# Gate and value of the state output from high and low parts, made by VectorE as the state output leaves its banks

## The reference, cut to what matters

```
y = jax.nn.gelu(s5_ssm(u, ...))              # (1, 1024, 256), "the state output"
ya, yb = jnp.split(y @ w_glu[l], 2, axis=-1) # w_glu: (256, 512)
o_ssm = ya * jax.nn.sigmoid(yb) * jax.nn.silu(z_ssm)
```

## Time and profile before

| | |
|---|---|
| median of 3 runs | 935.52 us (935.25 to 935.66) |
| profiled execution | 934.83 us, of which span 932.9 us |
| TensorE busy | 893.1 us, 96% |
| VectorE busy | 525.2 us, 56% |
| ScalarE busy | 416.9 us, 45% |
| GpSimd busy | 210.5 us, 23% |

### The profile page before, as it was taken

How to read it: one execution, slowest core, us unless ns; L and a number is a source line. 1 busy time by engine, 2 the same in 40 slices (tenths; PEclk the granted TensorE clock), 3 DMA queues, 4 the chain that set the end, 5 groups by cost and what they waited for, 6 DMA issues and landing times. The chain is left out here.

```text
span 932.9 us, 14437 instructions
## 1 busy us (share of the span) xinstructions
PE 893.1 (96%) x5577; PEld 735.0 (79%) x5577; DVE 525.2 (56%) x1098; ACT 416.9 (45%) x828; POOL 210.5 (23%) x203
## 2 busy tenths in 40 slices
PE   2799999999999999999999999999999999999997
PEld 2478999789999777777777776888888888887885
DVE  3652374359665697797798796732223122237454
ACT  6732232522345478778778768621111111133221
POOL 3359812111000103212212212255652000000000
PEclk9999999999999999999999999999999999999998
DMA  9956052041010000000000001333232121133222
GB/s 300 332 154 97 5 117 69 1 95 46 1 47 1 1 1 1 2 1 1 1 1 1 2 1 35 86 96 96 63 107 69 38 55 36 59 123 136 90 91 91
DMA packets 61092, 59.46 MB, mean 64 GB/s; under 512 B 10240, under 2 KB 53824, under 8 KB 61008
## 3 DMA queue, kind: packets, MB, share of 16 engines
q1 hardware_dynamic: 58768, 53.90, 20.1%
q0 software_dynamic: 2000, 4.54, 1.8%
q10 hardware_dynamic: 256, 0.09, 0.0%
HBM read 52.69 MB, written 5.24 MB: 62 GB/s over the span
## 5 line engine op out<-in xcount | busy, mean ns | idle before, releaser
L1240 DVE TENSOR_TENSOR plo<-pt,phi 128x512 fp32r<-128x512 f32 x192 | 106.2, 567 | 37.0 <-ACT phi L849 36.6
L849 ACT ACTIVATE pt<-bank 128x512 f32<-128x512 f32 (+1 forms) x208 | 99.6, 479 | 51.4 <-PE bank L1769 50.8
L1769 PE MATMUL bank<-q,k 128*128 128x512 f32 (+3 forms) x384 | 102.4, 348 | 0.4 <-ACT phi L849 0.4
L849 ACT ACTIVATE phi<-bank 128x512 fp32r<-128x512 f32 (+1 forms) x208 | 99.6, 479 | 0.0
L1769 PEld LDWEIGHTS bank<-q,k 128*128 128x128 f32 x384 | 63.0, 189 | 13.4 <-ACT phi L849 4.1
L648 POOL TENSOR_TENSOR qa<-qa,otmp 128x256 f32<-128x256 f32 x32 | 27.2, 851 | 198.4 <-DVE otmp L1240 198.4
L1562 DVE TENSOR_REDUCE mx<-slc_max 128x1 f32<-128x128 f32 (+3 forms) x64 | 48.2, 753 | 11.1 <-PE slc_max L1769 9.3
L1769 PE MATMUL bank<-ht_hi,dhi 128*128 128x512 f32 x128 | 49.8, 389 | 0.0
L1769 PE MATMUL bank<-ht_lo,dhi 128*128 128x512 f32 x128 | 49.8, 389 | 0.0
L1769 PE MATMUL bank<-ht_hi,dlo 128*128 128x512 f32 x128 | 49.8, 389 | 0.0
L1240 DVE TENSOR_TENSOR dtm<-bank,dsig 128x512 f32<-128x512 f32 x16 | 11.1, 691 | 64.4 <-ACT dsig L849 64.4
(11 more groups left out here) (445 smaller groups left out, 2600.6 us busy)
## 6 DMA issues: line engine op xcount, KB each, us to landing
ada<-in_w_ada SPq DMA_DIRECT2D x16, 512.0 KB, 10.1
draw<-in_w_in SPq DMA_DIRECT2D x16, 512.0 KB, 4.0
wraw<-in_w_in SPq DMA_DIRECT2D x7, 1024.0 KB, 5.7
xs<-in_x SPq DMA_DIRECT2D x8, 512.0 KB, 8.5
gstage<-in_w_ada POOLq DMA_DIRECT2D x16, 256.0 KB, 3.0
oraw<-in_w_out SPq DMA_DIRECT2D x8, 512.0 KB, 6.6
xr<-in_x SPq DMA_DIRECT2D x8, 512.0 KB, 4.2
out<-yr SPq DMA_DIRECT2D x7, 512.0 KB, 2.9
```

Of the source, the lines that this page charges most:

```text
L849: return nc.scalar.activation(o, i, fn, **kw)
L1240: return V.tensor_tensor(o, a, b, op)
L1769: return T.matmul(o, l, r, start=start, stop=stop, **kw)
```

## The change

TensorE's `glu` now makes each product from three pairs of fp32r matmuls (high weights x high output, low weights x high output, high weights x low output), twelve for a product where there were four in float32. VectorE makes the parts. In the step `("yt", 0)` it first makes those of the weights (`glu_weight_parts`: three copies, three subtractions), then in each step `("yt", q)` it waits for ScalarE's GELU of this quarter, copies it to `yt_hi` and writes `yt - yt_hi` to `yt_lo`, which lies in the place of `yt` itself (`state_rows_parts`). A new semaphore `early_lo`, which takes the place of `wlo0`, counts the first weights' low half, the weights' parts and the eight output parts, 10 in all. `glu(0)` waits for count 9 (the fourth high part) before its first matmul and for count 10 before its first matmul with a low output part. The wait of `glu(0)` for the weights' DMA moves to VectorE.

```diff
+    yt_hi = at("yt_hi", [P, 2, SEQ], R, R_K + 17408)
+    yt_lo = at("yt_lo", [P, 2, SEQ], R, R_Z)
+    wglu_hi = [[at("wglu_hi0", [P, 512], R, r_used - 2048)],
+               [at("wglu_hi1a", [P, 256], R, R_K + 16384), at("wglu_hi1b", [P, 256], R, R_K + 31744)]]
+    wglu_lo = at("wglu_lo", [P, 2, 512], R, R_K + 25600)
...
-                    .then_inc(once("wlo0") if half == 0 else s_wlo, 1)
+                    .then_inc(once("early_lo") if half == 0 else s_wlo, 1)
...
+            def glu_weight_parts():
+
+                dve.wait_ge(once("wglu"), 16)
+                pieces = ((0, 0, 0, 512), (1, 0, 0, 256), (1, 1, 256, 512))
+                for k, p_, c0, c1 in pieces:
+                    ch.mark(V.tensor_copy(wglu_hi[k][p_][:, :], wglu[:, k, c0:c1]))
+                ch.wait()
+                for k, p_, c0, c1 in pieces:
+                    ins = tt(wglu_lo[:, k, c0:c1], wglu[:, k, c0:c1], f(wglu_hi[k][p_][:, :]), ALU.subtract)
+                ins.then_inc(once("early_lo"), 1)
+
+            def state_rows_parts(q):
+
+                if q == 0:
+                    glu_weight_parts()
+                ctile, jh = divmod(q, 2)
+                part = lambda t: t[:, ctile, :].rearrange("p (n j) -> p j n", j=CH)[:, 4 * jh:4 * jh + 4, :]
+                dve.wait_ge(s_trf, first["yt"] + q + 1)
+                V.tensor_copy(part(yt_hi), part(yt)).then_inc(once("early_lo"), 1)
+                dve.wait_ge(once("early_lo"), 3 + 2 * q)
+                tt(part(yt_lo), part(yt), f(part(yt_hi)), ALU.subtract).then_inc(once("early_lo"), 1)
...
+                elif step[0] == "yt":
+                    state_rows_parts(step[1])
...
-                if n == 0:
-                    pe.wait_ge(once("wglu"), 16)
-                    pe.wait_ge(s_trf, first["yt"] + 4)
...
-                    for k in range(2):
-                        ins = mm(bank[2 + part], wglu[:, k, col:col + P], yt[:, k, cc * HALF:(cc + 1) * HALF],
-                                 k == 0, k == 1)
+                    w_high = (wglu_hi[0][0][:, col:col + P], wglu_hi[1][col // 256][:, col % 256:col % 256 + P])
+                    w_low = [wglu_lo[:, k, col:col + P] for k in range(2)]
+                    for m, (l, r) in enumerate(((w_high, yt_hi), (w_low, yt_hi), (w_high, yt_lo))):
+                        if n == 0 and part == 0 and m != 1:
+                            pe.wait_ge(once("early_lo"), 9 if m == 0 else 10)
+                        for k in range(2):
+                            ins = mm(bank[2 + part], l[k], r[:, k, cc * HALF:(cc + 1) * HALF],
+                                     m == 0 and k == 0, m == 2 and k == 1)
```

More of the change, by code:

```diff
@@ L1849, in _ @@
             pe.wait_ge(s_whi, 1)
-            pe.wait_ge(once("wlo0"), 1)
+            pe.wait_ge(once("early_lo"), 1)
             def state_input(k, cc):
```

## The result

The changed kernel takes 936.96 us (median of 19 runs, 935.96 to 937.97) beside 935.31 for the kernel before (19 runs, 934.89 to 936.45). The ratio is 1.0016 (95% interval 1.001 to 1.0023): 1.65 us slower, a change that can be told from none but lies within 0.2%. The spread of the changed kernel, 2.0 us, is wider. Its profiled execution took 935.99 us (span 934.2), near the lower end of its runs.

What follows compares the result with a forecast made beforehand. TensorE, busy 893.1 of 932.9 us, was taken to bound the kernel. A 4.5 us late start, less 2.84 gained, plus 1.7 for the clock made +3.4: 938.9 us, own range 937.5 to 940, wide range 933.3 to 940.6.

Steps and rivals of the forecast that it cites:

- the late start: TensorE's first product, waiting for VectorE's fourth high part, starts at 176.1 instead of 171.59: 4.5 us late.
- What is removed: On TensorE, twelve fp32r matmuls replace four float32 ones: 2.72 instead of 3.43 us a product, 2.84 for four.
- The weights' parts: VectorE's three copies and three subtractions for the weights end at about 168.1 in its hole and cost nothing.
- The subtraction: VectorE's subtraction for an output quarter, 512 elements at a step of 8 elements: 1.08 us.
- The copy: VectorE's copy of an output quarter, 512 elements at a step of 8 elements: 1.08 us.
- rival B: VectorE copies two elements at a time despite the step, 0.62 us: 935.5, or 937.2 with clock fall; chance 0.24.
- The clock: TensorE's pause of 4.3 us before the first product lets its clock fall to 1.2 GHz: 1.7 us lost.
- The sum: Over the whole kernel, 4.5 - 2.84 + 1.7 = +3.4 us, giving 938.9.
- The low part: TensorE's first product waits 0.2 us for the fourth low output part at full pace, not at the lower clock.
- C: The step costs VectorE nothing, copy 0.41 and subtraction 0.69 us: -2.2 us, 933.3; chance 0.18.
- C's dividing line: The change gains if VectorE's copy and subtraction for one output quarter take below some 1.9 us.
- Nothing downstream absorbs: No later TensorE wait in the stretch absorbs a shift; the hidden layer starts at 224.6, before 221.18.

Runs made afterwards that it cites:

- e3_warm: Changed kernel plus nine extra fp32r matmuls on TensorE ahead of the first product's wait, results overwritten: 935.32 us beside 935.06 for the kernel before.
- e5_gain: Kernel before with twelve fp32r matmuls a product; ScalarE writes the fp32r output itself, low output part left out: 932.26 us beside 934.88.
- e2_again: The changed kernel run once more, nothing altered: 937.08 us beside 935.06 for the kernel before.
- e6_wait: Changed kernel's VectorE instructions and first-product wait, but with the float32 products of the kernel before: 939.41 us beside 934.88 for the kernel before.
- e10_warm4: Changed kernel plus four extra fp32r matmuls on TensorE ahead of the first product's wait: 935.23 us beside 935.02 for the kernel before.
- e1_steps: Kernel before plus 13 VectorE copies and subtractions of 512 elements with various steps; only durations count: copy 0.42 in a row, subtraction 0.69.
- e4_rows: Changed kernel, VectorE splitting the output in contiguous halves, first product waiting for the third copy instead of the fourth: 932.51 us beside 935.06.
- e7_fill: Changed kernel with the projection of key tile 5 moved ahead of the first product on TensorE: 932.48 us beside 934.88 for the kernel before.
- e8_steps: Kernel before plus nine VectorE copies and subtractions of 512 elements with other steps; only durations count: all six subtractions 1.09 to 1.12 us.
- e9_both: Changed kernel with contiguous halves on VectorE and the projection of key tile 5 ahead of the first product: 932.18 us beside 935.02.

## Why the prediction was right in direction and off in size

Forecast were 938.9 us and +3.4; measured are 936.96 and +1.65. The direction holds, and so do the two mechanisms, a late copy and a fall of the clock; the size is twice too large. That the direction came out hangs on the clock. In the prediction the late start alone (4.5 us) outweighed the gain (2.84); measured, it doesn't (2.47), and with the clock kept up e3_warm is level with the kernel before. By the steps of the prediction:

- **What is removed.** A product in 2.72 us where it took 3.43: the second one measures 2.72, and e5_gain 2.62 us for the four with 2.84 forecast.
- **The weights' parts** end at 167.96 with 168.1 forecast and cost nothing.
- **The subtraction** at 1.08 us: 1.07 to 1.13.
- **The copy** at 1.08 us: here the prediction failed. It measures 0.62 to 0.67. I had both bounds and the right value, 0.62, under rival B, and took the rate of the subtraction because the nearest row with a step was a two-source instruction. The casts of the earlier trace rows had shown that a one-source instruction is not bound to that rate; the chance of 0.24 for B was too low. Four times 0.43 us too much, and 0.3 us of small sums, put the start of the first product at 176.1 instead of 174.06.
- **The clock.** Forecast was a fall in a pause of 4.3 us at 1.7 us; it fell in or behind one of 2.2 already and cost 1.5 and 1.7 us in two profiles, 1.8 between e2_again and e3_warm. That the price of 1.7 came out is in part luck: it was read from the pace of transposes in a stretch in which the granted clock on record stays 1.00. And the delay of 2.0 us from the earlier trace rows, by which a pause of 4.3 us was judged long, is 2.0 to 5.1 us in ten profiles. That the fall is not certain in so short a pause, for which B had half its chance, is not borne out: both profiles of the changed kernel and e6_wait's show it, e10_warm4's with its pause of 1.44 us doesn't.
- **The sum.** Rival B with the clock's fall was 937.2 us, 0.24 from the median; it had a chance of 0.12. The low part, which the prediction had waiting 0.15 to 0.2 us at full clock, is in time at the lower clock and late by 0.25 in e3_warm.
- **C**, that the step costs nothing, gave 933.3 and is refuted by e1_steps; built without the step, and with the finer wait, the change comes to 932.5 (e4_rows); by the estimate there, 933.6 with the old wait, near C's 933.3.
- **C's dividing line** was wrong: by it the change gains when a quarter takes under 1.9 us. A quarter took 1.70 and the change lost, because the line leaves out the price of the clock.
- **Nothing downstream absorbs**: the shift of 1.15 us at the hidden layer is the shift of the end. Its start, 222.33, is just above the 222 below which I had called myself wrong, and far from the 224.6 forecast.

The profiled execution shows only 1.15 us where the medians differ by 1.65. Its place among the runs (935.99 in 935.96 to 937.97) and e2's later fall of the clock point to the moment of the fall. The only trace of it in the other runs is their mean granted clock: in e2_again the five runs at 0.994 or 0.995 have a median of 937.52, the six at 0.996 or 0.997 one of 936.51. This mean also holds the low stretch at the end of the kernel, so it fits and does not show it.

## What to carry to other kernels

Work that moves to an idle engine is free only if its last piece is ready when the busiest engine asks for it: price the instruction in the access pattern it will have, one-source and two-source instructions apart, and split in the layout's contiguous direction where the producer's order leaves a choice. A new wait of TensorE of 2.2 us cost 4.5 us here (e6_wait), 2.6 for the later start and the rest for the clock that fell; a few independent matmuls put into the wait, useful ones or not, saved that second part. The moment of the fall varies, so one profile in which a pause did not lower the clock is weak evidence that it never will: the pause of 1.44 us was profiled once. When a change gains in one place and waits in another, build each half alone: here +4.5 and -2.6 us stood behind a difference of 1.65.

## What the runs showed that I had not expected

- A step of 16 or 32 bytes costs VectorE the same on either side and only once: 1.1 us for 512 elements with one, two or three stepped tensors, and 0.62 to 0.75 (once 0.93) for a copy, against 0.69 and 0.42 in a row. The stepped `pprod` of the earlier trace rows and its 1.79 ns an element fit this.
- VectorE's instructions with a step of 8 are slower beside fp32r matmuls (0.78 and 1.34 us in e3_warm, 0.75 and 1.20 in e7_fill, against 0.62 and 1.1 with TensorE idle), contiguous ones are not (0.42 and 0.69 in e4_rows beside the product), nor were e1's stepped subtractions beside the float32 product (1.08 to 1.11), nor the two copies with a step of 4 in e8_steps beside the projection (0.62).
- The clock can fall after the pause is over: in e2_again at 174.9, with the product running since 174.27, and in e6_wait at 175.5, with the product running since 174.21. In all three profiles it then stayed low for about 3.4 us.
- A product that starts as soon as VectorE's copy allows has its second matmul 0.34 us behind the first instead of 0.23, at full clock: behind pauses of 1.44 and 0.58 us in e10_warm4 and e3_warm, and in e4_rows and e7_fill without a visible pause. In e9_both, where the copy is there in time, it is 0.23.
